# Two layers of a diffusion backbone on one core: latent halves ahead of the context, and a share of expert work worked out for each run

## The reference

```python
hl = modulate(rms_norm(xl, lp['g_norm1']), mod_l[0], mod_l[1])
...
a_l = neighbourhood_attention(naq_l, nak_l, nav_l, ka_c, va_c, rpb)   # latents see the context's K, V
m_l = mla_latent(qn_l, qr_l, [kn_c, kn_l], [krr_c, krr_l], [vm_c, vm_l])
s_l = spatial_gating(uv_l, lp['sg_g'], lp['sg_w'], lp['sg_b'])
xl_new = xl + mod_l[2] * branch_merge(a_l, s_l, m_l, gate_l, w_branch, w_out)
...
h2 = modulate(rms_norm(xl_new, lp['g_norm2']), mod_l[3], mod_l[4])
xl_new = xl_new + mod_l[5] * peer_ffn(h2, ...)
```

```python
act = gelu(einsum('thkd,td->thk', exp_u[idx], hb))
out = einsum('thk,thkd->td', gate * act, exp_v[idx])
```

## Time and profile before

| | |
|---|---|
| median of 3 runs | 5908.52 us |
| profiled execution, in all | 5944.26 us |
| its span, first to last instruction | 5942.5 us |
| PE busy, DVE busy, POOL busy | 4593.6, 3052.5, 2750.7 us |
| granted TensorE clock, mean | 0.83 of full |
| transferred | 1651.91 MB, 278 GB/s over the span |

### The profile page before, as it was taken

The page is one execution under the profiler, slowest core; times in us unless marked ns, Lnnn a source line. Parts: engine busy times, 40 slices in busy tenths (PEclk is TensorE's granted clock), DMA queues, the critical chain, the costliest instruction groups (busy, mean ns, idle before and its releaser), DMA issues.

```text
span 5942.5 us, 57345 instructions
## 1 busy us (share of the span) xinstructions
PE 4593.6 (77%) x19168; PEld 2486.7 (42%) x19168; DVE 3052.5 (51%) x8176; ACT 1243.0 (21%) x3643; POOL 2750.7 (46%) x2566
## 2 busy tenths in 40 slices
PE   8998987788988878986755558999788798555555
PEld 4477543333664345552311115568534455111111
DVE  1213757865137766465665432421766646665642
ACT  1311223333112321121111012531232111111110
POOL 0001555655115545655676760000454466777674
PEclk8899988988988889997866668999888899666666
DMA  5554978977547878998998982114787799999997
GB/s 191 182 182 160 349 289 318 339 282 287 203 157 291 292 271 335 395 369 293 351 349 334 345 310 65 52 63 141 269 302 267 297 387 379 354 354 359 333 355 270
DMA packets 464131, 1651.91 MB, mean 278 GB/s; under 512 B 51169, under 2 KB 57441, under 8 KB 463841
## 3 DMA queue, kind: packets, MB, share of 16 engines
q0 software_dynamic: 368640, 1342.34, 61.3%
q1 hardware_dynamic: 95200, 305.90, 14.3%
HBM read 1645.94 MB, written 2.10 MB: 277 GB/s over the span
## 4 chain that ended last, share of the span: by engine, by line
PE 48%; POOL 13%; DVE 13%; DMA 12%; issue 10%; ACT 3%; another core or an unknown queue 1%; PEld 0%; SPq 0%; DVEq 0%; PEldq 0%; ACTq 0%; POOLq 0%
PE banks L646 15%; PE banks L924 12%; DMA vb<-in_peer_v_dram,idx 10%; POOL vb L1443 7%; POOL ub L1432 6%; DVE ub L1383 5%; PE banks L735 4%; PE banks L772 2%; PE banks L834 2%; PE banks L811 2%; PE banks L662 2%; PE banks L757 1%; PE banks L822 1%; DMA ub<-in_peer_u_dram,idx 1%; PE banks L896 1%
## 5 line engine op out<-in xcount | busy, mean ns | idle before, releaser
L924 PE MATMUL banks<-vb,dg 128*64 128x512 f32 x5120 | 1699.1, 796 | 865.9 <-DMA vb<-in_peer_v_dram,idx 771.0
L1432 POOL DMA_INDIRECT ub<-in_peer_u_dram,idx x1280 | 1430.5, 1118 | 1838.1 <-DVE idx L1371 1347.6
L1383 DVE CUSTOM_DVE_ANT_0 ub<-ub,h2cur 128x1024 f32<-128x1024 f32 x1280 | 1531.8, 1223 | 827.5 <-DMA ub<-in_peer_u_dram,idx 666.4
L1443 POOL DMA_INDIRECT vb<-in_peer_v_dram,idx x1280 | 1319.6, 1031 | 1334.2 <-PE banks L924 914.5
L924 PEld LDWEIGHTS banks<-vb,dg 128*64 128x64 f32 x5120 | 429.3, 169 | 1866.1 <-issue 1668.2
L646 PE MATMUL banks<-region,wring 128*128 128x256 f32 x3840 | 882.5, 390 | 30.9 <-ACT region L988 25.3
L646 PEld LDWEIGHTS banks<-region,wring 128*128 128x128 f32 x3840 | 739.0, 195 | 211.9 <-issue 101.9
L1134 ACT ACTIVATE dg<-consts,wgt 128x64 f32<-128x64 f32 x1280 | 358.8, 337 | 991.3 <-PE banks L924 402.8
L646 PE MATMUL banks<-h2T,wring 128*128 128x256 f32 x1280 | 312.9, 401 | 20.8 <-ACT h2T L988 20.8
L1326 DVE SCALAR_TENSOR_TENSOR region<-region,banks 128x256 f32<-128x256 f32 x120 | 50.5, 421 | 501.4 <-PE banks L646 485.6
L735 PE MATMUL banks<-region,wring 128*128 128x256 f32 (+1 forms) x1056 | 262.5, 405 | 49.7 <-ACT region L988 49.7
(11 more groups left out here) (146 smaller groups left out, 3962.5 us busy)
## 6 DMA issues: line engine op xcount, KB each, us to landing
wring<-w_gate_dram SPq DMA_DIRECT2D x120, 512.0 KB
wring<-w_mod_dram SPq DMA_DIRECT2D x96, 512.0 KB
wring<-w_pq_dram SPq DMA_DIRECT2D x80, 512.0 KB
wring<-w_branch_dram SPq DMA_DIRECT2D x60, 512.0 KB
wring<-w_out_dram SPq DMA_DIRECT2D x40, 512.0 KB
ub<-in_peer_u_dram,idx POOLq DMA_INDIRECT x1280
vb<-in_peer_v_dram,idx POOLq DMA_INDIRECT x1280
region<-in_na_rpb_dram SPq DMA_DIRECT2D x64, 256.0 KB
```

Of the source, the lines that this page charges most:

```text
L924: ins = nc.tensor.matmul(bank(ACC[a])[64 * g:64 * g + 64, :], dg[:, n % DG_RING, :], vb[:, n % V_RING, a * 512:(a + 1) * 512], start=first ...
L1383: nc.vector.tensor_tensor_reduce(out=ub[:, n % U_RING, :], in0=ub[:, n % U_RING, :], in1=h2cur[:, g, :], scale=1.0, scalar=0.0, op0=ALU.mu ...
L1432: pool.indirect_dma_start(ub[:, n % U_RING, :], None, u_rows, bass.IndirectOffsetOnAxis(ap=idx[:, u % IDX_RING, j:j + 1], axis=0)).then_in ...
L1443: pool.indirect_dma_start(vb[:, n % V_RING, :], None, v_rows, bass.IndirectOffsetOnAxis(ap=idx[:, u % IDX_RING, j:j + 1], axis=0)).then_in ...
```

## The change

Layer zero now starts with the context's keys and values only, then A and B through all stages, and then the context from its first stage on, its keys and values computed a second time (`again`). In layer one A and B do `kq_stage` first and the context's keys and values come behind them. `TILES` follows. The 24 modulation chunks of layer one stand in the merge of the context. `BG_STEP` is gone: the plan is made twice, first without background to find the costs at the marks, then with a step each `(cost between marks) / 128`. The marks lie behind the second score chunk of each `query_stage` and behind half B's `kq_stage` in layer one. The steps come to 3.34, 3.82, 1.52, (4.54, a run with nothing to gather), 3.34 and 0.44 units. Constants are stored in fewer columns, `modrow` has one buffer in place of two and a place of its own, `cS` too, and the ring of indices has 22 places.

```diff
-U_RING, V_RING, IDX_RING, DG_RING = 6, 4, 24, 8
+U_RING, V_RING, IDX_RING, DG_RING = 6, 4, 22, 8
...
-BG_STEP = 4.2
+SEL_KV, SEL_CQ, SEL_64, SEL_QK = 32, 64, 96, 128
+RUN = 128
...
-    ones = np.full((P, P), 1.0 / D, f)
+    ones = np.full((P, 1), 1.0 / D, f)
...
-        modrow = vb[:, 0, 0:512].rearrange("p (a n) -> p a n", a=2)
-        cS = vb[:, 0, 512:768].rearrange("p (k n) -> p k n", k=DK)
+        modrow = sb("modrow", [P, N])
+        cS = sb("cS", [P, DK, 32])
...
-        TILES = [(0, 0), (0, 1), (0, 2), (0, 3), (0, 4), (0, 5), (1, 2), (1, 3), (1, 4), (1, 5)]
+        TILES = [(0, 2), (0, 3), (0, 4), (0, 5), (0, 0), (0, 1), (1, 2), (1, 3), (1, 4), (1, 5)]
...
         def emit(step, cost=0.0):
             plan.append(step)
-            owed[0] += cost
-            while owed[0] >= BG_STEP:
-                owed[0] -= BG_STEP
+            pace["cost"] += cost
+            if pace["steps"] is None or not pace["marks"]:
+                return
+            step_cost = pace["steps"][len(pace["marks"]) - 1]
+            pace["owed"] += cost
+            while pace["owed"] >= step_cost:
+                pace["owed"] -= step_cost
                 if not bg_step():
-                    owed[0] = 0.0
+                    pace["owed"] = 0.0
+
+        def mark():
+
+            pace["marks"].append(pace["cost"])
...
-                    emit(("modr", l, c), 1.2)
                     if c not in (0, 8):
                         emit(("modt", l, c - 1), 0.4)
+                    emit(("modr", l, c), 1.2)
...
+            again = 1 if l == 0 and s == CTX_S and queries else 0
+            emit(("norm", l, s, "kq" if s or queries else "kc"), 6.0)
...
                 if cc:
                     emit(("sc", l, s, cc - 1), 0.8)
+                if cc == 2:
+                    mark()
                 if cc and cc % 2 == 0:
                     bgs["avail"] += 1
             bgs["avail"] += PH
...
+        def layer_tail(l, s):
+
+            mla_stage(l, s)
             fence()
+            if l == 0 and s == CTX_S:
+                mods.extend((1, c) for c in range(24))
+            merge_stage(l, s)
+            query_stage(l, s)
+            fence()
...
+            mods.extend((0, c) for c in range(8))
+            some_mods(8)
+            mods.extend((0, c) for c in range(8, 24))
+            kq_stage(0, CTX_S, False)
+            fence()
+            for l in range(LAYERS):
+                for s in (A_S, B_S):
+                    if l:
+                        until_tail(tile_no[(0, 2 * s + 1)])
+                    kq_stage(l, s, True)
+                    fence()
+                if l:
+                    mark()
+                    until_tail(tile_no[(0, 1)])
+                    kq_stage(l, CTX_S, False)
+                    fence()
+                na_stage(l, (A_S, B_S))
+                fence()
+                layer_tail(l, A_S)
+                layer_tail(l, B_S)
+                if l == 0:
+                    kq_stage(0, CTX_S, True)
+                    fence()
+                    na_stage(0, (CTX_S,))
+                    fence()
+                    layer_tail(0, CTX_S)
+            while steps is not None and bg_step():
+                pass
+
+        schedule(None)
+        marks = pace["marks"] + [pace["cost"]]
+        schedule([(b - a) / RUN for a, b in zip(marks, marks[1:])])
...
-                        ins = nc.tensor.matmul(bk[:, 2 * a:2 * a + 2], modrow[:, (cnt["mod"] - 1) % 2, a * P:(a + 1) * P], fold,
+                        ins = nc.tensor.matmul(bk[:, 2 * a:2 * a + 2], modrow[:, a * P:(a + 1) * P], fold,
```

More of the change, by code:

```diff
@@ L98, in program @@
         o += 82
-        sel_of = [consts[:, o + 66 * m:o + 66 * m + 66] for m in range(4)]
-        SEL_64, SEL_QK, SEL_KV, SEL_CQ = range(4)
-        smalls = sb("smalls", [P, LAYERS, 80])
+        sel = consts[:, o:o + 160]
+        smalls = sb("smalls", [P, LAYERS, 76])
         modraw = [smalls[:, l, 0:48] for l in range(LAYERS)]
-        gain_of = [smalls[:, l, 48:80] for l in range(LAYERS)]
+        gain_of = [smalls[:, l, 48:76] for l in range(LAYERS)]
         modcs = sb("modc", [P, LAYERS, 48, 2])
@@ L251, in program @@
         plan = []
-        owed = [0.0]
-        bgs = dict(avail=0, front=0, d=0, g=0, a=0, rate=1)
-        TILES = [(0, 0), (0, 1), (0, 2), (0, 3), (0, 4), (0, 5), (1, 2), (1, 3), (1, 4), (1, 5)]
+        pace = dict(owed=0.0, cost=0.0, marks=[], steps=None)
+        bgs = {}
+        TILES = [(0, 2), (0, 3), (0, 4), (0, 5), (0, 0), (0, 1), (1, 2), (1, 3), (1, 4), (1, 5)]
+        tile_no = {lt: n for n, lt in enumerate(TILES)}
         def topk_step():
             u, part = divmod(bgs["front"], 7)
+            assert part < 6 or bgs["a"] >= PAIRS * (u - IDX_RING + 1)
             bgs["front"] += 1
@@ L521, in query_stage @@
         def query_stage(l, s):
-            assert not mods or l or s
+            assert not [m for m in mods if m[0] == l]
             if bgs["avail"]:
@@ L569, in program, with schedule @@
-        while bg_step():
-            pass
+        def layer_tail(l, s):
+            mla_stage(l, s)
+            fence()
+            if l == 0 and s == CTX_S:
[3 more added lines that the diff above has]
+            fence()
+        def schedule(steps):
+            for a in (plan, loads, pace["marks"], bias_order, mods):
+                a.clear()
+            for a in (load_at, batches, units_of, bsb_no):
+                a.clear()
+            fences[0] = 0
+            pace.update(owed=0.0, cost=0.0, steps=steps)
+            bgs.update(avail=0, front=0, d=0, g=0, a=0, rate=1)
+            mods.extend((0, c) for c in range(8))
[15 more added lines that the diff above has]
+                na_stage(l, (A_S, B_S))
+                fence()
+                layer_tail(l, A_S)
[8 more added lines that the diff above has]
+                pass
@@ L650, in feature, with token_rows @@
                     last_by_bank(load, key)
-            def token_rows(l, s, what, src):
-                keys = [(l, s, what, t) for t in range(2)]
+            def token_rows(l, s, what, src, again=0):
+                keys = [(l, s, what, t, again) for t in range(2)]
                 bks = [fill(key) for key in keys]
                 for c in range(4):
-                    name = (l, s, what[0] if what == "vv" else "sv", c)
+                    name = (l, s, "v", c, again) if what == "vv" else (l, s, "sv", c)
                     w = weights(name)
@@ L755, in _ @@
                     which, q0, q1 = it["pick"][0]
-                    off = 32 - it["row"]
-                    ins = nc.tensor.matmul(bank(cnt["held"])[0:32, 0:N], sel_of[which][q0:q1, off:off + 32],
+                    off = which - it["row"]
+                    ins = nc.tensor.matmul(bank(cnt["held"])[0:32, 0:N], sel[q0:q1, off:off + 32],
                                            sq[q0:q1, i % 3, :], start=(i == 0), stop=(i == len(items) - 1),
@@ L780, in _ @@
                     emptied(pe, it["key"] + ("spread",))
-                    fills(nc.tensor.matmul(bk[64:96, 0:N], rot[64:96, 64:96], it["rope"], start=True, stop=True), key)
+                    fills(nc.tensor.matmul(bk[64:96, 0:N], rot[64:96, :], it["rope"], start=True, stop=True), key)
                     cnt["rope"] += 1
@@ L961, in _ @@
                     bk = whole(act, key)
-                    if cnt["mod"] >= 2:
-                        whole(act, mod_keys[-2])
-                    frees(nc.scalar.activation(modrow[:, cnt["mod"] % 2, :], bk[:, 0:256], ACT.Copy), key)
+                    if mod_keys:
+                        whole(act, mod_keys[-1])
+                    frees(nc.scalar.activation(modrow, bk[:, 0:256], ACT.Copy), key)
                     emptied(act, key)
@@ L1225, in _ @@
                     t0 = N * s
-                    rn = rn_mg if kind == "n2" else rn_of[s]
+                    rn = rn_mg if kind in ("n2", "kc") else rn_of[s]
                     if op == "norm":
```

102 lines of the change are left out of this document (36 added, 66 removed).

## The result

| | before | after |
|---|---|---|
| median, measured side by side | 5915.59 us | 6277.34 us (6261.24 to 6281.24) |
| ratio, 95% interval | | 1.0608 [1.0579, 1.0636] |
| span of the profiled execution | 5942.5 us | 6275.4 us |
| mean granted clock | 0.83 | 0.84 |

The changed kernel is 6.1% slower. I had forecast 1.6% slower, with 6120 us as the upper end; the time lies well above that.

The account below looks back on a forecast made before the run. Expert gathers were taken to bound stretches running them alone, 6.0 us a pair against 2.9 to 3.6 covered. Stages summed to 4911 us plus a 1129 us last stage, span 6040, median 6006; forecast 5950 to 6075, range 5845 to 6120.

Parts of the forecast that it names:

- the chains: Last query stage: six units run serially, top-k, gathers and sums without overlap, 78 us per 8 pairs; stage 1129 us.
- Step (2): Half A's query stage to half B's merge, both layers: 25 added pairs at 3.45 us each, 865 us.
- denser gathers gain nothing: Rival: half A's query to half B's merge, added pairs cost 6.0 us each, 930 us per copy; span 6170; chance 0.12.
- Step (3): Layer zero, half B's query stage (127 us), then context K, attention and latent attention: 481 us in all.
- step (5): Context query and layer one's K and Q of A and B, 133 dots and 144 sums: 900 us.
- step (4): Context merge with 59 pairs and 24 modulation chunks: 463 us by PE, 453 by bytes, taken as 465.
- the bandwidth rival: Wherever foreground work rides along, DMA carries 389 GB/s; span 5894, time 5860 us, faster than before; chance 0.14.
- (1): Start up to the first gathers, context K and V, then both latent halves: 794 us against 525 in before.
- (6): Layer one's stretch without gathers, context K and V through attention, latent attention and merge: 541 us.

Follow-up runs that it names:

- experiment 1: The changed kernel with 4.2 units a step in the last run alone: 5976.38 us, ratio 1.0232; with 4.2 in every run: 5946.54 us, ratio 1.0175.
- Experiment 6: Shares divided by 112 pairs, not 128: on the changed kernel with last run 4.2, ratio 1.0196; on before's order with shares run by run, 1.0054.
- experiments 4 and 7: Before unchanged, for its trace on another chip: 5840.73 us; before with the modulation steps swapped alone: 5878.19 us; before with one `modrow` buffer alone: 5845.64 us.
- experiment 7: Before's order, shares run by run, last 4.2, swap and single `modrow` undone: ratio 0.9862. Before with both edits: 1.0077; swap alone: 1.0078; single buffer alone: 1.001.
- experiment 3: The changed kernel with layer one's 24 modulation chunks back in the stretch without gathers at the start: 6183.6 us, ratio 1.0592.
- experiment 2: Before's order with early modulation, shares run by run and 4.2 units in the last, swapped modulation steps kept: 5814.66 us, ratio 0.9958 to before.

## Why the prediction was wrong

The direction was right, and so was the mechanism of the last stage: the chains, their length and their cost (1129 against 1134 us; experiment 1 gives them 3.7 points). What failed are terms of the sum ahead of it, the price of a pair, the start of a half with nothing in stock, and the rate of the dense stages; they cost 230 us.

**Step (2), the price of an added pair.** I took 3.45 us, the mean of the pairs that were there. Measured is (904 - 779)/25 = 5.0 us on the first chip and 5.1 in experiment 1. The mean had been read where DMA had more room; the merge of before ran at 336 GB/s, and the same merge in after, 395 us with 56 pairs, runs at 360 and a share of 0.94 (row below). My own rows held a dearer pair, which I left out: the second head group takes 85 us with 11 or 12 pairs against 37 without, 4.0 to 4.4 us each. The rival "denser gathers gain nothing" (6.0 each) was nearer than the forecast, but even its 930 us would have covered only 130 of the 235 us. I had given it 12%.

**Step (3), half B's query stage: 127 forecast, 173 measured.** The shares are worked out so that each run ends with its pairs used up. At the mark nothing is in stock, and top-k, index and first gathers of the next half stand in line behind its first scores with nothing beside them. I named this for a few microseconds in step (5) and put it at nothing here. Experiment 6 closes it and saves 42 us, about 30 of them once three fewer pairs are taken off. In the changed kernel POOL stands still there for its first indices:

```profile
1767.47 0.94 POOL L1463 DMA_INDIRECT ub<-in_peer_u_dram,idx  x1 [22.86 <-DVE idx L1402]
```

**Steps (4) and (5), the rate of a mixed stretch.** I used 389 GB/s in (4) as a bound and 352, the rate of gathers alone, in (5). Measured 351 and 325. The rows had it: the 800 us stretch of before, which is like (5), carried 326 GB/s. 314 MB at that rate are 963 us, and 964 were measured. I had used that row against the bandwidth rival and not in my own sum. By the bandwidth rival these stages would have carried 389; they didn't. The limit that the Trainium skill gives in "DMA: Bandwidth & Descriptors", section "Where 436 GB/s comes from", is about 358 GB/s a core. Half B's merge in layer one, 395 us long, ran close to it:

```profile
4746.00:5141.00 395.00, 320.50 (x1312) 190.64 (x1312) 205.90 (x516) 56.95 (x176) 245.04 (x222) 0.93 0.94 360
```

Stretches of before went beyond it, so it is no wall. As an estimate, the 176 MB of step (4) at that rate are 492 us, and 493 were measured; for step (5) it gives 877, further from the 964 than my 900. It is a guide for the merges and not for the mixed stretch. The clock in (5) was granted at 0.81 of full; what that adds to the 64 us there wasn't tried.

**Steps (1) and (6)** were off by 14 and 13 us and cancel. The 6 us at the start are there (the first stage begins at 46.3 us instead of 40.3), but not for the reason that I gave, the single `modrow`: on before the swap alone moves that stage from 41.0 to 46.2 us, the single buffer alone to 41.4 (experiments 4 and 7). And the sentence behind the sum, that the longer gap without gathers takes 71 us, misread the rows. Before's gap holds 80 us of half B's K and Q, which the change moves out of it, and is 550 us long; the changed kernel's is 528. The sum itself, 541, didn't use it.

**The median.** I scaled by 0.994, since the profiled execution of before was 0.6% over its median. The changed kernel's execution lies at its median. Of the 271 us between the forecast median of 6006 and 6277, 235 are the span's and 36 this scaling.

By factors, from the runs: shares run by run in the old order 0.986 (experiment 7); the swapped steps 1.010 there (0.9958/0.9862; 1.008 on before); the new order 1.0275; the last share 1.037. Each is the quotient of two neighbours in a row of kernels that leads from before to the changed one, so the product is the 1.061 measured by construction and confirms nothing; and the last one crosses chips. The factor of the order holds the first query stage, which begins at 805 us against 562 in experiment 2, the second pass over the context's keys and values, and the late modulation (about 36 us by experiment 3); its gap without gathers is the shorter one, 530 against 550 us. The new order was not run without the swap, so what the swap costs it beyond the 6 us at the start isn't known; against an old order without the swap it is 1.0232/0.9862 = 3.75% behind. How the rest of the 2.75% divides between the late start and the second pass wasn't tried.

## What to carry to other kernels

When work is moved under cover, don't price what is added at the mean of the work already there (3.45 us a pair here, against 5.0 measured): look at the bytes per second of the densest long stage, and price the stage by bytes at the rate of the row most like it. A share that uses up its stock at the end of a run leaves a hole at the border, about 30 us here; but filling it takes cover away elsewhere, and here it gained nothing clear. A share must not ask for more than becomes available while it runs: where production is limited, a greedy consumer turns a pipeline into a chain. And test each edit of a large change by itself; here one that looked like tidying cost 0.8%, and the best version (1.4% faster than before) is the old order with the change's pacing in all runs but the last, and without the swap.

## What the hardware showed beyond that

- PE can be busy for 59 of 60 us by its records, whose ends are modelled, and stay at 1.2 GHz all the time (three windows of the swapped kernel in experiment 7); with four small matmuls on the other side of sixteen it rises. The Trainium skill, "TensorE: Matmul & The Clock Gate", section "What's actually happening", has activity release the throttle; as far as busy time shows activity, this trace doesn't agree.
- The first chip ran before 1.3% slower than four others. One trace from it and one from another differ in stages with gathers alone: 781 against 800 us and 1013 against 1027, with 552 against 550 in the stretch without. The chained last stage, which mostly waits, took as long on the first chip (1134 us) as on another (1138).
